# Two blocks in one kernel: the pool stage and the first FFN of tokens 0 to 118 move into the expert stage, the other 137 tokens follow in plain float32

## The reference, cut to what matters

```python
# first block, last step: x is (256, 1024)
x = x + _peer(rmsnorm(x), ...)      # 256 tokens x 128 rows of peer_u and of peer_v
x = rmsnorm(x, normf_g)
# second block, layer 0 (pool)
y = pool_mixer(h)                   # per channel group: mean over tokens [t-w/2, t+w/2), w = 2,4,8,16,
x = x + g1 * y                      # minus the token, times a 256x256 matrix, for latent and context
u = h @ w_up                        # 1024 -> 2 x 2816
u = u[t-1]*cw[0] + u[t]*cw[1] + u[t+1]*cw[2] + cb
x = x + g2 * ((silu(a) * v) @ w_down)       # 2816 -> 1024
ctx = the same for the 256 context tokens   # layer 1 needs only its keys and values
```

## Time and profile before

| what | us |
|---|---|
| median of 3 runs | 1681.04 |
| lowest and highest of them | 1680.31, 1688.94 |
| the profiled execution's own time | 1669.39 |
| its span from first to last instruction | 1667.6 |

### The profile page before, as it was taken

One profiled execution on the slowest core, in us unless ns is written; L12 is line 12 of the kernel. 1 busy time (PEld: TensorE's weight loads), 2 busy tenths in 40 slices (PEclk: granted clock), 3 DMA queues, 4 the chain that ended last, 5 costly groups with the idle time before them and its releaser, 6 DMA issues.

```text
span 1667.6 us, 22193 instructions
## 1 busy us (share of the span) xinstructions
PE 1478.8 (89%) x8310; PEld 1059.6 (64%) x8310; DVE 1106.1 (66%) x2162; ACT 583.5 (35%) x847; POOL 824.9 (49%) x746
## 2 busy tenths in 40 slices
PE   8999999766565699999888885889999999999999
PEld 7997675654221266665443441438999896799987
DVE  4865633798488877877756675417886557468864
ACT  6653331211121222221100001127665454466652
POOL 0025230376767765656667777742675113036640
PEclk9999999987977899999799997999999999999999
DMA  7447860598999999999999999994555545635551
GB/s 281 152 151 301 318 253 26 210 389 304 393 407 371 409 401 402 402 403 403 401 401 394 409 396 402 406 396 161 171 187 190 189 182 222 243 111 202 176 191 38
DMA packets 154252, 477.15 MB, mean 286 GB/s; under 512 B 10017, under 2 KB 12321, under 8 KB 150945
## 3 DMA queue, kind: packets, MB, share of 16 engines
q0 software_dynamic: 73728, 268.47, 41.2%
q1 hardware_dynamic: 80416, 207.27, 34.0%
HBM read 474.65 MB, written 1.05 MB: 285 GB/s over the span
## 4 chain that ended last, share of the span: by engine, by line
PE 54%; DMA 13%; DVE 11%; POOL 10%; issue 5%; ACT 2%; DVEq 0%; ACTq 0%; POOLq 0%
PE ps L673 53%; DMA arena<-in_peer_v,cl 11%; POOL arena L2802 8%; DVE arena L1851 2%; PE ps L677 1%; POOL wring L2802 1%; DVE arena L1466 1%; DMA wring<-in_peer_v,cl 1%; DVE arena L1472 1%; DVE wring L1851 1%; DMA wring<-in_peer_u,arena 1%; DVE arena L1469 0%; DVE cvb L1472 0%; DVE arena L1781 0%; ACT arena L2190 0%
## 5 line engine op out<-in xcount | busy, mean ns | idle before, releaser
L673 PE MATMUL ps<-arena,wring 128*128 128x256 f32 (+2 forms) x2360 | 596.0, 488 | 106.0 <-DMA arena<-in_peer_v,cl 101.2
L673 PEld LDWEIGHTS ps<-arena,wring 128*128 128x128 f32 (+1 forms) x2360 | 333.0, 168 | 352.7 <-DMA arena<-in_peer_v,cl 179.7
L1851 DVE CUSTOM_DVE_ANT_0 arena<-arena 128x1024 f32<-128x1024 f32 x214 | 257.6, 1226 | 134.8 <-DMA arena<-in_peer_u,arena 131.9
L2802 POOL DMA_INDIRECT arena<-in_peer_u,arena x214 | 240.0, 1121 | 192.4 <-DVE arena L1809 78.2
L2802 POOL DMA_INDIRECT arena<-in_peer_v,cl x214 | 229.2, 1071 | 77.3 <-issue 60.4
L673 PE MATMUL ps<-hhl,wh 128*128 128x256 f32 (+1 forms) x1056 | 252.4, 323 | 1.2 <-POOL hhl L2812 0.7
L2190 ACT ACT_TABLE_LOAD x64 | 82.1, 1283 | 392.9 <-DVE arena L1851 266.1
L1466 DVE TENSOR_TENSOR wl<-wring,wh 128x2048 fp32r<-128x2048 f32 (+1 forms) x76 | 168.1, 2212 | 60.0 <-ACT wh L2193 58.2
L673 PE MATMUL ps<-hhl,wl 128*128 128x256 f32 x704 | 198.7, 282 | 0.0
L673 PEld LDWEIGHTS ps<-hhl,wh 128*128 128x128 f32 x1056 | 175.8, 190 | 19.5 <-POOL hhl L2812 2.5
L2193 ACT ACTIVATE wh<-wring 128x2048 fp32r<-128x2048 f32 (+1 forms) x78 | 146.1, 1874 | 70.7 <-PE ps L673 68.9
(11 more groups left out here) (257 smaller groups left out, 2025.4 us busy)
## 6 DMA issues: line engine op xcount, KB each, us to landing
wring<-in_ups SPq DMA_DIRECT2D x33, 2048.0 KB, 9.2
wring<-in_ada SPq DMA_DIRECT2D x24, 2048.0 KB, 9.9
wring<-in_ffn_w_down SPq DMA_DIRECT2D x12, 2048.0 KB, 9.0
wring<-in_w_in SPq DMA_DIRECT2D x8, 2048.0 KB, 8.3
wring<-in_ffn_w_down SPq DMA_DIRECT2D x6, 1536.0 KB, 7.6
wring<-in_peer_wq SPq DMA_DIRECT2D x4, 2048.0 KB, 16.1
wring<-in_attn_w_qkv SPq DMA_DIRECT2D x4, 2048.0 KB, 8.4
wring<-in_w_out SPq DMA_DIRECT2D x2, 2048.0 KB, 9.7
```

The costliest lines, as they stand in the source:

```text
L673: return pe.matmul(o, l, r, start=start, stop=stop)
L1851: ve.tensor_tensor_reduce(out=o, in0=o, in1=h2[:, t, :], scale=1.0, scalar=0.0, op0=MUL, op1=ADD, accum_out=dots[j % 2][:, k:k + 1]).then_ ...
L2802: po.indirect_dma_start(out=ring[n % NR], out_offset=None, in_=table, in_offset=bass.IndirectOffsetOnAxis(ap=which, axis=0)).then_inc(S[f" ...
```

## The change

The order of the expert stage's context work is new, and part of the 256 tokens' own work joins it.

- Tokens 0 to 118 (the last one only for the convolution: column 119) stand in one array `wide_h` behind the context's 256 columns and a column of zeros: 377 columns. Up blocks 0 to 5 (`EARLY_BLOCKS`) run for the context alone (256 columns, kind `ctx`), from count 182, one per 15 gathers. From count 311 on, when `v_add` 1 is there, the pool stage runs for tokens 0 to 118, then up blocks 0 to 5 for these tokens alone (kind `a`, 120 columns; their weights are loaded a second time), then up blocks 6 to 21 for both at once (kind `both`, 377 columns, 5.6 gathers each), then the down products for both (376 columns).
- PE takes four rows of `peer_v` at a time in place of two (`m % 4 == 3`).
- After the last gather the pool stage and the FFN run for the rest: 136 columns in the pool products, 138 in the up products, 137 in the down products, all in plain float32. The splitting into high and low parts, the three products and POOL's part in it are gone for layer 0.

```diff
+    EARLY_BLOCKS = 6
+    WIDE, FROM_A, LAST_A = 377, 257, 376
+    wide_h = area(OWN + 2048, 8 * WIDE).rearrange("p (c n) -> p c n", c=8)
+    B0, NB = 118, 138
+    VISITS = [(f, "ctx") for f in range(EARLY_BLOCKS)] + [(f, "a") for f in range(EARLY_BLOCKS)]
+    VISITS += [(f, "both") for f in range(EARLY_BLOCKS, 22)] + [(f, "b") for f in range(22)]
+    COLS = {"ctx": (0, 256), "a": (FROM_A, WIDE), "both": (0, WIDE)}
...
+    def step_places():
+        places = [5 * (k + 1) // 2 for k in range(11)] + [44 + 56 * (k - 10) // 10 for k in range(11, 34)]
+        n = 182
+        for f in range(EARLY_BLOCKS + 2):
+            places.append(n)
+            n += 15 if f < EARLY_BLOCKS else 2
+        n = max(n, 311)
+        for lengths in ([1.5] * 14, [2.2] * EARLY_BLOCKS, [5.6] * (22 - EARLY_BLOCKS), [1.5] * 2,
+                        ([2.7] * 8 + [2.1] * 4) * 2, [1.2] * 11):
...
-                elif n >= (4 * (steps + 1) if steps < 11 else 44 + 56 * (steps - 10) // 10):
+                elif steps < len(places) and n >= places[steps]:
...
         load("poolc", ("p_cpl", 4), pool_w(), n=3)
+        for g in range(EARLY_BLOCKS // 2):
+            load(("cup", "ctx", g), ("p_cu", 2 * g + 2), up(0, g), n=3)
+        sp.wait_ge(*at("v_cpl", 4))
+        sp.dma_start(area(AFTER, 1568), a["c_bands"]).then_inc(S["d_l"], 16)
+        sp.wait_ge(*at("v_idx", 8))
+        sp.dma_start(nfb_a, a["normf_g"].partition_broadcast(128)).then_inc(S["d_g2"], 16)
+        load("poola", ("p_pla", 4), pool_w(), n=3)
         for g in range(11):
-            load(("cup", g), ("p_cu", 2 * g + 2), up(0, g), n=3)
+            load(("cup", "both", g), ("p_cu", EARLY_BLOCKS + 2 * g + 2), up(0, g), n=3)
...
+            def visit(v):
+                f, kind = VISITS[v]
+                c0, c1 = COLS[kind]
...
                 for i in range(2):
                     for kk in range(8):
+                        k = mm(b[i], wu[:, kk, i, c128(f % 2)], wide_h[:, kk, c0:c1], kk == 0, kk == 7)
...
-                            k = mm(bs[m][:, 0:256], w[:, f, c128(m)], actT[:, f0 + f, :], f0 + f == 0, f0 + f == 21)
+                            k = mm(bs[m][:, 0:LAST_A], w[:, f, c128(m)], wide_act[f0 + f][:, 0:LAST_A], f0 + f == 0, f0 + f == 21)
...
-                elif what[0] == "use" and ROWS[what[1]][0] == "v" and ROWS[what[1]][2] % 2 == 1:
+                elif what[0] == "use" and ROWS[what[1]][0] == "v" and ROWS[what[1]][2] % 4 == 3:
...
-                        for k in range(m - 1, m + 1):
+                        for k in range(m - 3, m + 1):
...
+        def ffn_b():
+            token_norms(1)
+            for f in range(22):
...
+                for i in range(2):
+                    for kk in range(8):
+                        k = mm(b[i], w[:, kk, i, c128(f % 2)], sqb[:, kk, B0:256], kk == 0, kk == 7)
...
+                            k = mm(bs[m_][:, 0:NB - 1], w[:, f, c128(m_)], act_b[f0 + f], f0 + f == 0, f0 + f == 21)
...
-        ffn(0, 0, 1)
+        ffn_b()
```

More of the change, by code:

```diff
@@ L1292, in ffn @@
             for n in range(22):
-                b = where["up", l, n] = [take(("up", l, n, i), "v_up", 22 * l + n + 1) for i in range(2)]
+                b = where["up", l, n] = [take(("up", l, n, i), "v_up", n + 1) for i in range(2)]
                 if n == 0:
@@ L2502, in context @@
+            told(k, "a_sza", 1)
+            yield
+            yield
+            for q in range(2):
+                ac.wait_ge(*at("p_xT", q + 1))
+                for j in range(4):
+                    c = 4 * q + j
+                    k = actf(xA[:, c, :], where["xT", 0, q][:, 128 * j:128 * j + 128], ACT.Identity, bias=PB[:, 0, c:c + 1])
+                told(k, "a_mb", q + 1)
+            yield
+            for _ in range(3):
                 yield
+            yield from modulated_c(2, lambda c: wide_h[:, c, FROM_A:WIDE], 0, 1, 0)
```

628 lines of the change are left out of this document (413 added, 215 removed).

## The result

The changed kernel takes 1730.21 us (median of 4 runs, 1726.92 to 1732.26), the kernel before on the same chip 1684.94 us (4 runs). The ratio is 1.0286, 95% interval 1.0254 to 1.0318: slower by 48 us by the ratio (the two medians lie 45 us apart). Forecast were 1700 us, 19 us slower, with a range up to 1728 us. The direction is right, the size is not.

What follows compares the result with a forecast made beforehand. Transfers bound the expert stage before, PE the FFN behind; after the change PE would bound the expert stage's second half. -41 + 122 - 56 - 6 = +19 us, 1700 us median; range 1664 to 1728 us.

Steps and rivals of the forecast that it cites:

- First half: Expert stage up to `v_add` 1: fewer weight loads, a gain of 41 us (bounds 25 to 45).
- Early pool stage and kind `a`: Start of the expert stage's second half: 27 us paced by gathers, then 38 us bound by transfers.
- Wide blocks and down products: Expert stage after `v_add` 1: PE is the bound, 283 us of matmuls plus 38 us of expert rows, 321 us.
- The check from the other side: Expert stage from `v_add` 1 on, summed from PE's earlier busy time and its changes: 434 us, beside 428.
- Item 4: End of the expert stage: last `peer_v` rows, context's norms, keys and values; PE 37 us, transfers 42, so 42 us.
- Late pool stage: Pool stage after the last gather: 18 us in place of 24.0, 6 less (bounds 3 and 9).
- FFN behind: FFN after the last gather: 528 plain float32 matmuls, PE the bound, 132.5 us (127 to 142) in place of 189.0.
- 122: Expert stage from `v_add` 1 on: a loss of 122 us, 428 us in place of 305.6.
- the -62: After the last gather: a gain of 62 us, 56 in the FFN and 6 in the pool stage.
- The rival of the hidden wide blocks: Expert stage stays bound by transfers throughout: -40 us, 1641 us; chance 0.17 together with a halfway case.
- that of the two pairs' price: Expert rows on PE: four rows cost two pairs, +52 us, 1752 us; chance 0.10.

Runs made afterwards that it cites:

- the spread: Changed kernel with the key and value weights' load issued early and more gathers per wide up block and down step: 1705.66 us, ratio 1.0137.

## Why the prediction was wrong, step by step

- **First half, -41 us: right.** -43 to -47 us compared like with like (sum at 766.46 to 770.72 in kernels with the same first half, before 813.40).
- **Early pool stage and kind `a`, 27 + 38 = 65 us: the sum nearly right by luck,** 40 + 30 = 70 us. PE's hand-overs made the first of them longer than its bound above (37 us), with 22.5 us of waits. The second was said to be bound by 38 us of transfers; it is bound by PE, busy 28 of 30 us. That its loads had landed during the first is likely, but no run shows it.
- **Wide blocks and down products, 321 us: right, and for the reason given.** 324 us; a record of 377 columns takes 165.8 / 512 = 0.324 us (said 0.3275), a set of four 1.86 us (said 1.9). Narrowed columns give 272 us at 392 GB/s. The check from the other side was no proof: it gave 434 us of PE's work for the whole half, and the trace has 409 us busy and 48 idle.
- **Item 4, the rest, 42 us: this step failed.** It was taken as the larger of 42 us of transfers and 37 us of PE, as if they ran side by side. It took 63.5 us, at 280 GB/s with PE busy 47. The bytes were right, 280 GB/s over 64 us are 17.9 MB or some 44 us at 402 GB/s; the overlap was not there. The prediction named that the keys and values "wait for the last of these", but not that the expert rows stand behind them on PE: while PE waits 12.53 us and then computes keys and values for 16 us, no buffer of a gather comes free, and POOL waits 22.04 us for PE. First PE waits for a transfer, then the transfers for PE, then PE for the gathers. Issuing the load early took 6 us off the rest, and 7 to 8 off the distance of the two sums; with fewer rows left for the rest as well, the two sums came 37 us closer, 13 of which came back behind them. That the late load is a part of the cause is shown by a run. That the taking of turns is the remainder is read from the changed kernel's trace and agrees with the spread, where five sets fewer made the rest 30 us shorter and the wide part no longer; but some 9 us of these 30 are products that moved behind the sum, and no run takes the turns away alone.
- **Late pool stage, 18 us: wrong in size, 27.8 us.** The prediction scaled the rows of before by columns. Three of its products don't scale: windows 3.97 us (before 2.12) and map 5.61 us (said 3.8), both at a lower clock (0.50 and 0.70 granted, before 1.00): PE stands idle 5.94 and 2.03 us ahead of them, where before the gaps were 1.39 and 0.73 us (in traces where the map runs faster it takes 3.94 us, what the forecast said); norm sums 5.95 us (before 3.73), since a stationary operand of 10 columns and one of 128 take turns. That is 5.9 of the 9.8 us over; of the remaining 3.9, 2 are the shortening of DVE's and ACT's work that was taken and did not come, and 1.3 the longer wait ahead of the map.
- **FFN behind, 132.5 us: better than said, 125.0 us** (first matmul 1263.47 to the norm sums at 1388.47). 1056 records take 0.119 us each, not the 0.1255 scaled from the earlier trace rows, and it fell below the lower bound of 127.

The sum, compared like with like: -43 to -47, + 151, - 57 make +47 to +51 us against +19; the ratio gives +48. The 151 are 122 with 5 more for the first two items, 3 for the third and 21 for the fourth. The -57 is not the -62: 64 gained in the FFN, 4 lost in the pool stage, 3 in what follows.

Four terms lay outside their bounds: the early pool stage (40 us, up to 37 said), the rest (63.5, said 30 to 42), the late pool stage (27.8, said 15 to 21) and, on the good side, the FFN (125.0, said 127 to 142). The rest was farthest out, by 21 us, the late pool stage by 7. Both ends of the rest assumed that PE and the transfers overlap; the serial sum, 42 + 37 = 79 us, was the end that was missing. The rival of the hidden wide blocks was wrong as argued (transfers at 331, not 400 GB/s), and so was that of the two pairs' price. A slip of reading changed nothing: the slices of the earlier trace rows over the expert stage lie at 394 to 409 GB/s, not up to 411.

## What to carry to other kernels

Where work of several engines is joined in one stretch, its length is the larger of their busy times only if each queue holds something else to do while one instruction waits. Go through the in-order queues of the stretch and add what stands behind each wait; take the serial sum of the busy times as the upper end. A small remainder behind a long stretch that PE fills is worth laying inside it while the transfers have room: here that gave 12 to 17 us.

## What the runs showed of the hardware

- Two stationary operands in turn, of 10 and of 128 columns, cost 5.95 / 32 = 0.186 us for a record of 128 moving columns in plain float32; the same 32 records grouped by width 3.81 / 32 = 0.119 us. Two operands of 128 columns in turn, in the kernel before, took 3.73 us. The 10 and 128 in turn took 5.95 or 5.96 us in every trace that has them, whether the map before them took 3.94 or 5.61 us. The Trainium skill, TensorEngine Tiling (Array Packing), Key Properties, says that a change of the tiling mode drains the engine. Whether going from 128 to 10 columns is such a change, no run here shows.
- Expert rows on PE, each an operand of 32 columns, cost by the visit: one pair 1.84 us, two pairs back to back 1.87 us, four rows in one set 1.86 us, each time up to the next full weight load.
- The granted clock after gaps isn't a property of the kernel alone: the same map behind a gap of 1.7 to 2.1 us took 3.94 us (clock 1.00) in some traces and 5.61 us (0.70) in others, on the same kernel. Fourteen small matmuls ahead brought the windows from 3.97 to 2.09 us in one kernel, and to 3.50 and 3.97 us in two others.
- The same kernel ran at two speeds on different occasions: the same first half of the expert stage ended at 766 to 771 us with 398 to 404 GB/s on some and at 775 to 782 us with 384 to 390 GB/s on others. Whether that is the chip isn't shown; one and the same chip number stands beside groups of both kinds. Ratios beside the kernel before, taken together with it, take that out, differences between traces don't.
